# A fused decoder step in float32: VectorE's order in two attention stretches, and a broadcast row that a DMA spreads

## The reference

```
xn = RMSNorm(x);  one projection of xn gives mLSTM q, k, v, o, i, f, the MLA query and key latents, and both gates
h  = x + W_out( sig(g_A) * W_A(mLSTM(xn)) + sig(g_B) * W_B(MLA(xn)) )
y  = h + ConvFFN(RMSNorm(h))
# MLA, per head:   s = q k^T * scale; p = softmax(s + mask); o = (p c_kv) W_uv
#   q and k are normalised per row over nope and rope parts (qk_norm)
# mLSTM, per head: w = exp(min(a_s - m_t, mask)), with m the running maximum of a
#   num = (q k^T * w) v + w_state * q C;  h = num / max(|den|, exp(-m))
```

## Time and profile before

| what | us |
| --- | --- |
| median of 3 runs | 2963.84 (2960.9 to 2964.82) |
| the profiled execution's own time | 2965.1 |
| its span in the trace | 2963.2 |
| PE busy | 2902.8 (98% of the span) |
| DVE busy | 1430.0 (48%) |
| ACT busy | 1142.6 (39%) |
| DMA queue of SP and the engines' DMAs | 356.44 MB, 40.6% of 16 DMA engines |
| granted TensorE clock, mean | 0.991 of 2.4 GHz |

### The profile page before, as it was taken

How to read it: one execution, slowest core, us unless ns; L and a number is a source line. 1 busy time by engine, 2 the same in 40 slices (tenths; PEclk the granted TensorE clock), 3 DMA queues, 4 the chain that set the end, 5 groups by cost and what they waited for, 6 DMA issues and landing times. The chain is left out here.

```text
span 2963.2 us, 49885 instructions
## 1 busy us (share of the span) xinstructions
PE 2902.8 (98%) x19414; PEld 2701.2 (91%) x19414; DVE 1430.0 (48%) x2174; ACT 1142.6 (39%) x1883; POOL 105.3 (4%) x346
## 2 busy tenths in 40 slices
PE   8998999999999998999999999999999999999999
PEld 7855898988898896899999999999999999999999
DVE  5464432333333332354545444445676754677644
ACT  5536332332232231344444333333444433444433
POOL 0000000000000000000000000002100000000000
PEclk9999999999999998999999999999999999999999
DMA  6522301001001102656565655556555555655564
GB/s 208 203 73 83 116 1 33 17 17 33 21 12 33 33 1 93 196 153 201 159 187 170 190 161 169 163 152 193 169 163 168 155 152 169 180 168 159 147 180 128
DMA packets 619380, 370.95 MB, mean 125 GB/s; under 512 B 23793, under 2 KB 600883, under 8 KB 618169
## 3 DMA queue, kind: packets, MB, share of 16 engines
q1 hardware_dynamic: 607032, 356.44, 40.6%
q10 hardware_dynamic: 11824, 11.50, 1.1%
q0 software_dynamic: 368, 0.81, 0.1%
HBM read 345.98 MB, written 22.75 MB: 124 GB/s over the span
## 5 line engine op out<-in xcount | busy, mean ns | idle before, releaser
L286 DVE TENSOR_TENSOR w_lo_b<-stage,w_hi_b 128x2048 fp32r<-128x2048 f32 (+1 forms) x289 | 619.1, 2142 | 430.0 <-ACT w_hi_b L279 429.9
L298 PE MATMUL bank<-xnH,w_hi_b 128*128 128x288 f32 x2784 | 756.4, 299 | 6.0 <-PEq L191 5.9
L299 PE MATMUL bank<-xnL,w_hi_b 128*128 128x288 f32 x2784 | 751.0, 297 | 0.0
L279 ACT ACTIVATE w_hi_b<-stage 128x2048 fp32r<-128x2048 f32 (+1 forms) x289 | 517.8, 1792 | 571.8 <-PE bank L303 536.3
L298 PEld LDWEIGHTS bank<-xnH,w_hi_b 128*128 128x128 f32 x2784 | 524.6, 188 | 18.4 <-issue 18.1
L299 PEld LDWEIGHTS bank<-xnL,w_hi_b 128*128 128x128 f32 x2784 | 524.4, 188 | 0.3
L1517 PE MATMUL bank<-ukH,latH 128*128 128x384 f32 (+2 forms) x1280 | 457.9, 358 | 0.0
L1519 PE MATMUL bank<-ukH,latL 128*128 128x384 f32 (+2 forms) x1280 | 452.3, 353 | 0.0
L1518 PE MATMUL bank<-ukL,latH 128*128 128x384 f32 (+2 forms) x1280 | 451.8, 353 | 0.0
L1748 DVE TENSOR_REDUCE rk<-sq_n 128x3 f32<-128x384 f32 (+1 forms) x320 | 184.8, 579 | 508.0 <-ACT sq_n L1672 508.0
L303 PE MATMUL bank<-xnH,w_lo_b 128*128 128x288 f32 x2784 | 396.5, 295 | 0.0
(11 more groups left out here) (474 smaller groups left out, 2799.4 us busy)
## 6 DMA issues: line engine op xcount, KB each, us to landing
stage<-in_w_in_dram SPq DMA_DIRECT2D x88, 1024.0 KB, 5.2
stage<-in_w_up_dram SPq DMA_DIRECT2D x88, 1024.0 KB, 5.4
stage<-in_w_down_dram SPq DMA_DIRECT2D x64, 704.0 KB, 4.5
latf<-in_cache_kv_latent_dram SPq DMA_DIRECT2D x64, 256.0 KB, 2.5
stage<-in_w_branch_a_dram SPq DMA_DIRECT2D x16, 1024.0 KB, 5.6
stage<-in_w_branch_b_dram SPq DMA_DIRECT2D x16, 1024.0 KB, 5.5
stage<-in_w_out_dram SPq DMA_DIRECT2D x16, 1024.0 KB, 5.6
stage<-in_w_uk_dram SPq DMA_DIRECT2D x8, 1024.0 KB, 5.2
```

The source lines that it names most:

```text
L279: act.activation(h, a, ACT.Copy).then_inc(w_hi, 1)
L286: dve.tensor_tensor(lo, a, h.bitcast(F32), ALU.subtract).then_inc(w_lo, 1)
L298: pe.matmul(out, hi, xH(k), start=first and k == 0, stop=False)
L299: pe.matmul(out, hi, xL(k), start=False, stop=False)
```

## The change

The change has three parts, in the order of the program.

1. Queries and keys on DVE. `uq_low(2)` moves ahead of `latent(1)` and `key_rope`; each later `uq_low` stands behind a `rotated`, as before. `low_part(j)` moves ahead of `key_norm` and `key_inverse` in its step. The reciprocals of the last three pairs move: pair 5 behind step 18, pairs 6 and 7 behind the first two heads' softmax. In place of one wait for all 8 reciprocals, `soft(h)` waits for its own pair's.
2. The row of maxima. `neg_MT` is stored once to an internal DRAM tensor, by SP just ahead of the `hb_scratch` store. SP then reads one row per head, broadcast to 128 partitions, into one of two slots of `nmb`.
3. The ones matmul (L2050) and ACT's `nmr` (L2135) are gone, with their semaphores. DVE reads `nmb` in SBUF in place of bank 6, and a new semaphore `qk` tells it that the product of queries and keys is ready.

```diff
+    nm_dram = nc.dram_tensor("nm_scratch", (AH, T), F32, kind="Internal").ap()
...
+                    uq_low(2)
                     latent(1, ckvT, G_KVA)
                     key_rope()
                     for p in range(PAIRS):
-                        if p + 2 < PAIRS:
-                            uq_low(p + 2)
                         rotated(p)
+                        if p + 3 < PAIRS:
+                            uq_low(p + 3)
...
+                        if h >= 10 and (h - 10) % 4 == 0:
+                            low_part((h - 10) // 4)
                         if h >= 3 and h % 2 and h < BH + 2:
                             key_norm((h - 3) // 2)
-                        if h >= 6 and h % 2 == 0:
+                        if 6 <= h < BH and h % 2 == 0:
                             key_inverse(h // 2 - 3)
-                        if h >= 10 and (h - 10) % 4 == 0:
-                            low_part((h - 10) // 4)
-                    key_inverse(PAIRS - 1)
+                    key_inverse(PAIRS - 3)
...
-                    dve.wait_ge(k_rc, PAIRS)
...
                         s_ = sm[:, h % 4, :]
+                        dve.wait_ge(k_rc, h // 2 + 1)
                         dve.wait_ge(e_s, h + 1)
...
                     norm_(0)
                     norm_(1)
+                    key_inverse(PAIRS - 2)
+                    key_inverse(PAIRS - 1)
...
+                    sp.wait_ge(nm_made, 1)
+                    sp.dma_start(nm_dram, neg_MT[:]).then_inc(nm_out, 16)
                     sp.wait_ge(f_hev, 2)
...
+                        if h.i is None and h.c == 0:
+                            sp.wait_ge(nm_out, 16)
+                        need(sp, H["w"], h.of(3, -3))
+                        sp.dma_start(nmb[:, a, :], nm_dram[bass.ds(h.of(), 1), :].broadcast_to([P, T])).then_inc(nm_in[a], 16)
...
-                            pe.wait_ge(H["nmr"], h.of(1, 1))
-                            need(pe, H["csu"], h.of(NB))
-                            pe.matmul(bank[6][:, 0:T], ones[0:AH, :], nmr[:], start=True, stop=True).then_inc(H["nm"], 1)
...
-                            need(act, H["nm"], h.of())
-                            act.activation(nmr[:], neg_MT[:], ACT.Copy, scale=ident[0:AH, bass.ds(h.of(), 1)]).then_inc(H["nmr"], 1)
...
-                            dve.wait_ge(H["nm"], h.of(1, 1))
-                            nm_ = bank[6]
+                            dve.wait_ge(nm_in[a], h.div(2, 1, 16))
+                            need(dve, H["sc"], h.of(2))
+                            nm_ = nmb[:, a, :]
...
+                            dve.wait_ge(H["qk"], h.of(1, 1))
```

More of the change, by code:

```diff
@@ L1327, in build @@
         xn_back = lasting("xn_back")
+        nm_made, nm_out = lasting("nm_made"), lasting("nm_out")
         with ExitStack() as ph:
@@ L1871, in gates @@
                             dve.wait_ge(g_m, 1)
-                            dve.tensor_scalar(neg_MT[:], MT[:, 0, :], -1.0, None, ALU.mult)
+                            dve.tensor_scalar(neg_MT[:], MT[:, 0, :], -1.0, None, ALU.mult).then_inc(nm_made, 1)
                         if j == 4:
@@ L1958, in build @@
             sc_ = sb(ph, "sc_m", [P, 4 * P])
-            nmr = sb(ph, "nmr", [AH, T])
+            nmb = sb(ph, "nmb", [P, 2, T])
             qm = sb(ph, "qm", [P, NB, N_S])
@@ L1971, in build @@
             n_tr = sb(ph, "n_tr", [AH + NB * AH, P])
-            names = ("t kw vc0 vc1 nmr nm w ex sc qm km num ds dn rd hn sq rt r2 hs ht y H L cp cpe cs csu nc ncp nall one fin").split()
+            names = ("t kw vc0 vc1 qk w ex sc qm km num ds dn rd hn sq rt r2 hs ht y H L cp cpe cs csu nc ncp nall one fin").split()
             H = {x: sem("h_" + x) for x in names}
             c_in = [sem("c_in0"), sem("c_in1")]
+            nm_in = [sem("nm_in0"), sem("nm_in1")]
             c_out = [sem("c_out0"), sem("c_out1")]
@@ L2046, in step @@
                             pe.matmul(bank[5][:, S_P:3 * P], kT_[:, a, P:S_P], qT_[:, a, P:S_P], start=True, stop=True)
-                            pe.matmul(bank[5][0:N_S, 3 * P:3 * P + N_S], kT_[:, a, S_P:T], qT_[:, a, S_P:], start=True, stop=True)
-                            pe.wait_ge(H["nmr"], h.of(1, 1))
-                            need(pe, H["csu"], h.of(NB))
-                            pe.matmul(bank[6][:, 0:T], ones[0:AH, :], nmr[:], start=True, stop=True).then_inc(H["nm"], 1)
+                            pe.matmul(bank[5][0:N_S, 3 * P:3 * P + N_S], kT_[:, a, S_P:T], qT_[:, a, S_P:], start=True, stop=True).then_inc(H["qk"], 1)
                         if j == 2:
```

## The result

The first comparison gave 2945.72 us (median of 4 runs, 2944.86 to 2953.18) against 2963.12 for the kernel before (median of 4, 2960.9 to 2964.82): a ratio of 0.9947, 95% interval 0.9935 to 0.9959. That is faster, as forecast, but by 17.4 us of the medians (15.6 us of the means) where the sum said 12.7.

What follows compares the result with a forecast made beforehand. PE, busy 98% of the span, bounds the kernel: only its work, waits and clock count. 1.76 (queries) + 4.9 (key waits) + 1.64 (clock) + 4.8 (ones matmul) - 0.4 (DMAs) = 12.7 us, from 2963.84 to 2951.1 us; range 2946.5 to 2957.0.

Steps and rivals of the forecast that it cites:

- All five statements: PE's waits: none before third pair or `absorbed`, about 1.2 us before step 17's transposes, under 0.5 before `absorb`, 6.3 behind barrier.
- Queries: PE's third query pair: its 1.76 us idle time goes with the low part put first; bounds 0.6 and 1.8 us gained.
- the cover of 1.9 us: Queries: slack left between the next low part, done at 107.9, and PE wanting it at about 109.8.
- Clock: Keys' end and first values: low clock behind the 3.29 us wait goes, 1.64 us gained; bounds 0 and 1.64.
- The rule that spoke against it: Keys: transposes do not count as busy PE for the clock, so it could fall anyway; sum 1.64 us smaller.
- That rival: Keys' stretch: the clock falls anyway, through new waits or transposes; 11.1 us gained, 2952.8 us; chance 0.15.
- the mis-sized term: mLSTM, L2050 gone: 0.6 us in each of eight slots, 4.8 us gained; bounds 3.6 and 5.4.
- the barrier's 0.4 us: SP ahead of the mLSTM barrier: the added `neg_MT` store costs 0.4 us; bounds 0.2 and 1.0.
- Late reciprocals: Softmax: pairs 6 and 7 inverted after head 1, covered by DVE's idle time; cost nothing, bounds 0 and 1.8 us lost.
- The rival that the cover fails: Softmax and first rotated query late on PE, 1.8 + 1.2 us lost; 9.7 us gained, 2954.1 us; chance 0.10.
- The slower rival: mLSTM: broadcast read comes late, delaying DVE and PE's block; 2.3 us per head for example gives 2969.8 us; chance 0.02.
- It only moves the waits: Keys' stretch ends where it did; only the ones matmul's 4.8 us less 0.4 gained, 2959.4 us; chance 0.07.

Runs made afterwards that it cites:

- the keys' part alone: Kernel before with only low parts ahead of the reciprocals in the keys' steps and the last three reciprocals late: 2956.75 us median of 10, ratio 0.9979.
- the low parts alone: Kernel before with only the low parts ahead of key_norm and key_inverse, all eight reciprocals in their places: 2959.42 us, one run.
- the late reciprocals alone: Kernel before with only the last three reciprocals late, low parts still behind the reciprocals: 2954.81 us, one run.

## Why the prediction was right

- **Waits.** All five statements on them held: no idle time before the third pair; `absorbed` without a wait; 1.27 us before the transposes of step 17 (1.2 forecast); 0.27 us before `absorb` (0.35); 6.3 us behind the barrier (6.3). From the first matmul of the keys to the last `absorb` PE is 5.2 us faster with the keys' part alone (4.9 forecast). It came out so near because each wait was followed to the next one on paper, with DVE's durations from the trace. Taking the waits off without that gives 6.6 us, 1.4 too much.
- **Queries.** 1.76 us forecast, 1.8 in the traces and 1.7 (0.2 to 3.1) by means; the cover of 1.9 us held.
- **Clock.** 1.64 us was put down for it as certain in the sum. Five of six profiles with the wait pay it, so on average it is worth about 1.4 us, an estimate (5/6 of 1.64). The prediction's reading that this wait brings the clock down is right only as a tendency. The keys' part measured 6.2 us (4.2 to 8.2) against 4.9 + 1.64 = 6.5.
- **The rule that spoke against it.** The new waits stand among transposes, and after them the granted clock is 1.00 in each of the three profiles of the changed kernel. By the Trainium skill, page "TensorE: Matmul & The Clock Gate", section "Part 4: PE-mode transpose", such a stretch could have fallen to the lower level; these traces do not show it, and the keys' part alone has the same waits and a clock of 1.00 too. That rival is out in all four.
- **The ones matmul: the mis-sized term.** The step "some of the 0.68 us may be the change-over to the block and stay" was wrong: the 0.18 us left from L2059 to the block are those that stood between the product and L2050 before (1249.78 - 1249.60). The whole 0.68 us is gone, 0.68 x 8 = 5.4 us in place of 4.8. The upper bound held. With the barrier's 0.4 us that is 5.0, and 5.9 (3.9 to 7.8) was measured. The estimate of 0.49 us from the Trainium skill ("TensorE: Matmul & The Clock Gate", section "Back-to-back issue gap", and "FP8 and Floating Point Precision", section "TensorE Precision Notes") is 0.19 us too low for this matmul of 8 rows.
- **Late reciprocals.** They cost nothing: `soft(2)` starts behind them, PE's `turn_p` does not wait. The rival that the cover fails is out.
- **Broadcast reads.** They land in at most 7.0 us and nobody waits for `nmb`. The slower rival is out.
- **"It only moves the waits".** False of the whole, and of each half: the low parts alone gave 2.0 us, the late reciprocals alone 3.2. Only 1.5 of the 3.3 us that the low parts took away came back at the next copies.

With the terms as the traces show them the sum is 1.8 + 5.2 + 1.4 + 5.4 - 0.4 = 13.4 us, against 13.3 measured (11.4 to 15.3). The forecast sum of 12.7 is 0.7 us short of that: the waits were put 0.3 us and the ones matmul 0.6 us too low, the clock 0.2 us too high. The range was too narrow at its low end for a median of 4 runs. It allowed 2 us for what such medians differ by, from three runs of before; the two groups 4 to 7 us apart make that more.

## What to carry to other kernels

When an engine off the path sits in the way with long instructions, follow each awaited result to the last wait of the stretch: moving a step forward brings part of the wait back at the next result, here 1.5 of 3.3 us. To gain the rest, something must leave the stretch, and what leaves must find idle time behind (here DVE's 4.80 us in the softmax). A step that only a later stage needs should not stand between two copies that the bound engine waits for; one of 3.35 us there cost 3.2 us of wait, and 1.7 us of clock besides. With times in two groups, compare means of ten or more runs, or read the gain off the distance between two landmark instructions in each trace. A single start time misleads, as the same work starts up to 1.3 us earlier or later from one profile to the next.

## What the runs showed of the hardware

- The granted clock falls to its lower level at a wait of 3.3 to 3.5 us of PE in most executions (five of six) and not in all, and the same program loses 13.4 or 21.8 us of clock in the same two stretches from one execution to the next.
- On SP the two stores ahead of the barrier took 2.91 and 0.65 us, the one store before 3.18. With the small store moved 27 us ahead, away from the weight loads, it took 0.33 us and the other one 2.97. So the 3 us are paid by whichever comes first behind the weight loads; the further small store in the same place adds 0.4.
- Removing a float32 matmul of 8 rows and 288 columns ahead of a block frees 0.68 us, all of the time from its start to the block's; the change to the block's matmuls costs nothing that is seen.
- The first query matmul of PE, ahead of every change, starts between 89.84 and 91.13 us in the twelve profiles.
